# Second convolution buffer, and a new order of the top-k rounds, block adds and sums on VectorE, in a hybrid SSD and sparse attention layer

## The reference, cut to what matters

```python
proj = h @ w_in                                   # (T, 9064)
z, xbc, dt_raw, q, k, v, qi, ki, wi, g = jnp.split(proj, split_points, axis=-1)
xbc, conv_new = causal_conv(xbc, conv_state, conv_w, conv_b)   # 4 taps for each channel
xbc = jax.nn.silu(xbc)
xs, Bm, Cm = jnp.split(xbc, (SSM_INNER, SSM_INNER + SSM_GROUPS * SSM_STATE), axis=-1)
dt = jax.nn.softplus(dt_raw + dt_bias);  A = -jnp.exp(A_log)
y_ssd, ssm_new = ssd_scan(xs, dt, A, Bm, Cm, ssm_state, 64)    # needs the running sums of dt * A
y_ssd = rmsnorm((y_ssd + D_skip * xs) * jax.nn.silu(z), ssm_norm_g)
...
_, sel = lax.top_k(iscore, topk)                  # keys of each query row: 128 or 256
o = softmax(q @ k[sel]) @ v[sel]
...
x = x + (gate_a * (y_ssd @ w_ssm_out) + gate_b * (o @ w_attn_out)) @ w_o
x = x + HierMoE(rmsnorm(x))
```

## Time and profile before

| | us |
|---|---|
| median of 3 runs (1522.3 to 1525.94) | 1523.73 |
| the profiled execution, its own time | 1521.15 |
| its span in the trace | 1519.5 |
| TensorE busy in the span | 1350.7 (89%) |
| VectorE busy | 784.1 (52%) |
| ScalarE busy | 492.6 (32%) |
| GpSimd busy | 229.1 (15%) |

### The profile page before, as it was taken

How to read it: one execution, slowest core, us unless ns; L and a number is a source line. 1 busy time by engine, 2 the same in 40 slices (tenths; PEclk the granted TensorE clock), 3 DMA queues, 4 the chain that set the end, 5 groups by cost and what they waited for, 6 DMA issues and landing times.

```text
span 1519.5 us, 19482 instructions
## 1 busy us (share of the span) xinstructions
PE 1350.7 (89%) x7202; PEld 903.1 (59%) x7202; DVE 784.1 (52%) x1707; ACT 492.6 (32%) x1155; POOL 229.1 (15%) x334
## 2 busy tenths in 40 slices
PE   7989789999999999987788899999999969878880
PEld 5545466666676766765565677777765545444440
DVE  3158877878878878878655621101113533211105
ACT  2143124665654655534655420000002211111112
POOL 3000000220320321222530000000000023222210
PEclk9999999999999999999999999999999979988995
DMA  8412332435444435344019425203215199999975
GB/s 262 121 30 54 85 111 94 135 105 161 135 127 130 145 97 139 107 147 111 17 26 193 156 94 159 56 0 116 106 53 241 65 356 414 415 416 415 414 293 215
DMA packets 148176, 247.45 MB, mean 163 GB/s; under 512 B 39540, under 2 KB 106852, under 8 KB 139156
## 3 DMA queue, kind: packets, MB, share of 16 engines
q1 hardware_dynamic: 137012, 215.10, 42.1%
q0 software_dynamic: 11072, 31.12, 6.0%
HBM read 216.50 MB, written 36.88 MB: 167 GB/s over the span
## 4 chain that ended last, share of the span: by engine, by line
PE 47%; DVE 7%; ACT 3%; issue 3%; DMA 2%; POOL 1%; SPq 0%; DVEq 0%; POOLq 0%; ACTq 0%
PE psum L1413 14%; PE psum L1680 9%; PE psum L662 9%; PE psum L1580 5%; PE psum L1696 4%; PE psum L1417 3%; DVE arena L2277 1%; ACT arena L1993 1%; PE psum L1398 1%; ACT arena L1915 1%; PE psum L1317 1%; DVE arena L2716 1%; PE psum L1362 1%; POOL arena L1116 1%; DMA wring<-in_w_in 1%
## 5 line engine op out<-in xcount | busy, mean ns | idle before, releaser
L662 PE MATMUL psum<-hT,wring 128*128 128x320 f32 x1024 | 296.9, 442 | 29.2 <-DVE arena L627 17.4
L662 PEld LDWEIGHTS psum<-hT,wring 128*128 128x128 f32 x1024 | 195.9, 194 | 116.4 <-DVE arena L627 18.9
L662 PE MATMUL psum<-wring 128*128 128x320 f32 x768 | 218.2, 434 | 0.0
L662 PEld LDWEIGHTS psum<-wring 128*128 128x128 f32 x768 | 146.4, 191 | 61.9 <-issue 1.0
L1417 PE MATMUL psum<-ident,arena 128*128 128x128 f32 (+3 forms) x950 | 139.6, 284 | 41.0 <-ACT arena L1915 11.5
L1417 PEld LDWEIGHTS psum<-ident,arena 128*128 128x128 f32 (+3 forms) x950 | 105.2, 143 | 94.8 <-issue 61.9
L1413 PE MATMUL psum<-arena,wring 128*128 128x320 f32 x512 | 138.1, 431 | 0.0
L1413 PEld LDWEIGHTS psum<-arena,wring 128*128 128x128 f32 x512 | 96.6, 189 | 41.2
L638 ACT ACTIVATE wring<-psum 128x320 f32<-128x320 f32 (+2 forms) x140 | 49.6, 379 | 188.7 <-PE psum L662 178.0
L1680 PE MATMUL psum<-wring,arena 128*64 128x256 f32 x608 | 84.3, 439 | 23.8 <-issue 21.0
L1915 ACT ACTIVATE arena<-psum 128x512 f32<-128x512 f32 (+8 forms) x155 | 71.7, 517 | 83.9 <-PE psum L1417 57.1
(11 more groups left out here) (344 smaller groups left out, 1940.9 us busy)
## 6 DMA issues: line engine op xcount, KB each, us to landing
wring<-in_w SPq DMA_DIRECT2D x38, 1024.0 KB, 21.6
arena<-in_w SPq DMA_DIRECT2D x32, 1024.0 KB, 24.7
wring<-in_w_in SPq DMA_DIRECT2D x25, 1024.0 KB, 5.5
oT<-in_w SPq DMA_DIRECT2D x14, 1024.0 KB, 21.8
hT<-in_w SPq DMA_DIRECT2D x12, 1024.0 KB, 20.5
arena<-a_rows SPq DMA_DIRECT2D x20, 512.0 KB, 4.0
arena<-in_state_ssm SPq DMA_DIRECT2D x16, 512.0 KB, 7.3
out<-arena POOLq DMA_DIRECT2D x16, 512.0 KB, 3.8
```

Of the source, the lines that this page charges most:

```text
L662: ins = nc.tensor.matmul(o[:, 0:TH], wt[:, k, :], rows[:, k, :], start=n in (1, 5, 2) and k == 0, stop=k == 3, skip_group_check=True)
```

## The change

Seven edits stand in it, all in the order or the buffers, none in what is computed:

- The taps of odd tiles j go to a second buffer, the first 664 columns of `xdt` (the scan's product buffer, idle at that time). `conv(u)` waits for `silu(u - 2)` rather than `silu(u - 1)`; the tile j = 1 of groups 1 to 3 waits until the scan of the group before has read `xdt` and its state has been written from there; the first product into `xdt` waits for `silu(5)`.
- `sums_of_a` stands on VectorE directly behind block (0, 0) of x1 in group 0, no longer behind the rounds and adds of x1, and TensorE's products for it stand between the first four and the last three steps of x1. ScalarE's part moves up likewise.
- The pair x0 of group 0 uses bank 5 rather than bank 3 for its steps 1, 6, 7 and 4.
- In `sum_rows` the wait for the indexer's query product stands before the one subtraction that overwrites hT, and no longer ahead of all four.
- The rounds between the adds of q 3 and of x0 of group 0 are gone or behind the adds.
- In the first gates the adds of block (0, 0) come ahead of the rounds, and `sum_weights` of gb 0 behind the first of them.
- The tables of rounds: 39 of 80 are done when group 0 begins (45 before), then 54, 59, 64 and 69 at the ends of the groups (54, 58, 62, 66 before), and 11 in the gates (14 before).

```diff
--- before.py
+++ after.py
@@ -43,9 +43,9 @@
 TOPK_P, TOPK_S = 128, 256
 ROUNDS_P = TOPK_P // 8
 ROUNDS = 3 * ROUNDS_P + TOPK_S // 8
-TOP_Q = (24, 27, 34, 38, 43)
-TOP_GROUP = (45, 54, 58, 62, 66)
-TOP_GATES = (70, 75, 79, ROUNDS)
+TOP_Q = (24, 27, 32, 39)
+TOP_GROUP = (39, 54, 59, 64, 69)
+TOP_GATES = (71, 73, 75, 77, 79, ROUNDS)
 CHUNK = 64
 PAIRS = SMP * AR
 ATT_SCALE = HD ** -0.5
@@ -232,18 +232,20 @@
 def plan_group(b, g):
 
     lo, hi = (0, 1, 2, 3), (4, 5, 6, 7)
-    plan_pair(b, ("x", g, 0), (3, 1, 2), SEVEN[:4])
+    x0_banks = (3 if g else 5, 1, 2)
+    plan_pair(b, ("x", g, 0), x0_banks, SEVEN[:4])
     if g:
         b.add(("yt", g - 1), (0,))
     b.add(("cT", g), (7,))
-    plan_pair(b, ("x", g, 0), (3, 1, 2), SEVEN[4:])
-    plan_pair(b, ("x", g, 1), (0, 1, 2))
+    plan_pair(b, ("x", g, 0), x0_banks, SEVEN[4:])
+    plan_pair(b, ("x", g, 1), (0, 1, 2), SEVEN[:4])
     if g == 0:
         for tt in range(NT):
             b.add(("ac", tt), hi)
             b.add(("ae", tt), hi, readers=2)
         for i in range(2):
             b.add(("ar", i), hi)
+    plan_pair(b, ("x", g, 1), (0, 1, 2), SEVEN[4:])
     plan_pair(b, ("bc", g), (3, 1, 2))
     plan_pair(b, ("z", g, 0), (0, 1, 2))
     b.add(("cO", g, 0), (7,))
@@ -438,6 +440,7 @@
         czero = ebs[:, SMP % 2, 0:2 * P].rearrange("p (u t) -> p u t", u=2)
         dec = ebs[:, SMP % 2, 2 * P:2 * P + 4 * SB].rearrange("p (j b) -> p j b", j=4)
         sout = xdt[:, 1, :]
+        taps = [acc[:, 0, :], xdt.rearrange("p u n -> p (u n)")[:, 0:664]]
         arow = ebs.rearrange("p u n -> p (u n)")[0:HEADS, 0:T]
         mt_f = mt.rearrange("p u n -> p (u n)")
 
@@ -678,12 +681,12 @@
         def sum_rows(dve):
 
             tt_ = nc.vector.tensor_tensor
-            wait_full(dve, ("qiS",))
             tt_(row_sums[0], top_r, top_l, ALU.subtract).then_inc(S["sums_ready"], 1)
             dve.wait_ge(S["sums_ready"], 5)
             tt_(row_sums[1], low_r, row_sums[0], ALU.subtract).then_inc(S["sums_ready"], 1)
             dve.wait_ge(S["sums_ready"], 6)
             tt_(row_sums[2], low_l, row_sums[1], ALU.subtract).then_inc(S["sums_ready"], 1)
+            wait_full(dve, ("qiS",))
             tt_(top_r, low_r, top_r, ALU.subtract).then_inc(S["sums_ready"], 1)
 
         def wait_chunk(pe, key):
@@ -1157,7 +1160,7 @@
                 ins = turn(o[:, 24 * j:24 * (j + 1)], cin[0:24, j, :], 24)
             filled(ins, ("cT", g))
             dense(pe, ("x", g, 0), SEVEN[4:])
-            dense(pe, ("x", g, 1))
+            dense(pe, ("x", g, 1), SEVEN[:4])
             if g == 0:
 
                 pe.wait_ge(S["a_ready"], 1)
@@ -1174,6 +1177,7 @@
                         ins = mm(o[0:HEADS, (tt - 4 * i) * P:(tt - 4 * i + 1) * P], av[:, tt, :],
                                  (cum_p if tt < SMP else cum_s)[:], start=True, stop=True)
                     filled(ins, ("ar", i))
+            dense(pe, ("x", g, 1), SEVEN[4:])
             dense(pe, ("bc", g))
             dense(pe, ("z", g, 0))
 
@@ -1747,9 +1751,9 @@
                 ct = 4 * g + j if j < 4 else 16 + g if j == 4 else 20 + g
                 dst = xsT[:, j, :] if j < 4 else bcT[:, j - 4, :]
                 act.wait_ge(S["conv_done"], 6 * g + j + 1)
-                fn(dst[:, 0:TP], acc[:, 0, 0:TP], ACT.Silu, bias=cb_col[:, ct:ct + 1])
+                fn(dst[:, 0:TP], taps[j % 2][:, 0:TP], ACT.Silu, bias=cb_col[:, ct:ct + 1])
                 fn(dst[:, TP:T].rearrange("p (b q) -> p b q", q=SQ),
-                   acc[:, 0, 512:664].rearrange("p (b q) -> p b q", q=19)[:, :, 3:19], ACT.Silu,
+                   taps[j % 2][:, 512:664].rearrange("p (b q) -> p b q", q=19)[:, :, 3:19], ACT.Silu,
                    bias=cb_col[:, ct:ct + 1]).then_inc(S["xs_ready"], 1)
 
             if g == 0:
@@ -1763,11 +1767,7 @@
                 squares_act(act, g - 1, fn)
             stage_(x1_, 6)
             silu(0)
-            stage_(x1_, 5, 7)
-            if g:
-                gains_act(act, g - 1, fn)
-            silu(1)
-            raws(x1_, 2)
+            stage_(x1_, 5)
             if g == 0:
                 for tt in range(NT):
                     wait_read(act, ("ae", tt), 1)
@@ -1777,6 +1777,11 @@
                 fn(w2v, w2v, ACT.Exp).then_inc(S["a_exp"], 1)
                 copy(("ar", 0), arow[:, 0:512], bank(("ar", 0))[0:HEADS, :])
                 copy(("ar", 1), arow[:, 512:T], bank(("ar", 1))[0:HEADS, 0:P])
+            stage_(x1_, 7)
+            silu(1)
+            if g:
+                gains_act(act, g - 1, fn)
+            raws(x1_, 2)
             stage_(bc, 1)
             silu(2)
             stage_(bc, 6)
@@ -2091,9 +2096,12 @@
                 ct = 4 * g + j if j < 4 else 16 + g if j == 4 else 20 + g
                 dve.wait_ge(S["raw_ready"], u + 1)
                 wait_read(dve, key + (3,))
-                if u:
-                    dve.wait_ge(S["xs_ready"], u)
-                a, r = acc[:, 0, :], raw[:, j % 2, :]
+                if u >= 2:
+                    dve.wait_ge(S["xs_ready"], u - 1)
+                if j == 1 and g:
+                    wait_full(dve, ("yo", g - 1, SMP))
+                    dve.wait_ge(S["sout_written"], 16 * g)
+                a, r = taps[j % 2], raw[:, j % 2, :]
                 link(ts_(a, r[:, 0:664], cw_col[:, 0, ct:ct + 1], None, ALU.mult))
                 for w in range(1, CW):
                     ins = stt(out=a, in0=r[:, w:w + 664], scalar=cw_col[:, w, ct:ct + 1], in1=a, op0=ALU.mult, op1=ALU.add)
@@ -2109,17 +2117,19 @@
                     dve.wait_ge(S["gathered"], u - 1)
                 pair_added(dve, key, block)
 
+            def sums_of_a():
+
+                for tt in range(NT):
+                    wait_full(dve, ("ac", tt))
+                    release(nc.vector.tensor_copy(acv[:, tt, :], bank(("ac", tt))[:, 0:HEADS]), ("ac", tt))
+                    wait_full(dve, ("ae", tt))
+                    wait_read(dve, ("ac", tt))
+                    release(tt_(w2v[:, tt, :], bank(("ae", tt))[:, 0:HEADS], acv[:, tt, :], ALU.subtract), ("ae", tt))
+
             tops = TOP_GROUP[g], TOP_GROUP[g + 1]
             rounds = [tops[0] + (tops[1] - tops[0]) * i // 4 for i in range(5)] if g == 0 else \
-                [tops[0], tops[0], tops[0] + 1, tops[0] + 2, tops[1]]
+                [tops[0], tops[0] + 1, tops[0] + 2, tops[0] + 3, tops[1]]
             for i, (key, nxt) in enumerate(((("x", g, 0), ("x", g, 1)), (("x", g, 1), ("bc", g)), (("bc", g), ("z", g, 0)))):
-                if i == 1 and g == 0:
-                    for tt in range(NT):
-                        wait_full(dve, ("ac", tt))
-                        release(nc.vector.tensor_copy(acv[:, tt, :], bank(("ac", tt))[:, 0:HEADS]), ("ac", tt))
-                        wait_full(dve, ("ae", tt))
-                        wait_read(dve, ("ac", tt))
-                        release(tt_(w2v[:, tt, :], bank(("ae", tt))[:, 0:HEADS], acv[:, tt, :], ALU.subtract), ("ae", tt))
                 conv(key, 2 * i)
                 conv(key, 2 * i + 1)
                 if i == 2 and g:
@@ -2129,6 +2139,8 @@
                         raws_added(nxt, 2 * i + 2, block)
                     else:
                         pair_added(dve, nxt, block)
+                    if block == (0, 0) and i == 0 and g == 0:
+                        sums_of_a()
                     if block == (0, 0):
                         sum_weights(dve, (("bc", g), ("z", g, 0), ("z", g, 1))[i])
                         top(rounds[i], rounds[i + 1])
@@ -2138,6 +2150,8 @@
                     tt = step
                     k = NT * g + tt
                     wait_full(dve, ("xt", g, tt))
+                    if tt == 0:
+                        dve.wait_ge(S["xs_ready"], 6 * (g + 1))
                     if tt >= 2:
                         wait_full(dve, ("yo", g, tt - 2))
                     elif tt == 0 and g:
@@ -2213,16 +2227,18 @@
             for block in ((0, 0), (1, 1), (0, 1)):
                 pair_added(dve, nxt, block)
             if g == GROUPS - 1:
-                sum_weights(dve, ("gb", 0, 0))
                 for i, key in enumerate((("ga", 0, 1), ("gb", 0, 0), ("gb", 0, 1))):
-                    top(TOP_GATES[i - 1] if i else TOP_GROUP[-1], TOP_GATES[i])
                     if i == 2:
                         dve.wait_ge(S["squares_added"], GROUPS)
-                    for block in ((0, 0), (1, 1), (0, 1)):
-                        pair_added(dve, key, block)
+                    pair_added(dve, key, (0, 0))
+                    if i == 0:
+                        sum_weights(dve, ("gb", 0, 0))
+                    top(TOP_GATES[2 * i - 1] if i else TOP_GROUP[-1], TOP_GATES[2 * i])
+                    pair_added(dve, key, (1, 1))
+                    pair_added(dve, key, (0, 1))
                     if i == 0:
                         sum_weights(dve, ("gb", 0, 1))
-                top(TOP_GATES[2], TOP_GATES[3])
+                    top(TOP_GATES[2 * i], TOP_GATES[2 * i + 1])
```

(5 more changed lines are left out.)

## The result

| | before | after |
|---|---|---|
| median of the runs measured together, us | 1524.84 | 1504.12 |
| lowest and highest | 1522.3 to 1527.42 | 1500.83 to 1505.47 |
| the profiled execution, its own time | 1521.15 | 1503.05 |
| its span | 1519.5 | 1501.4 |

The ratio is 0.9865, 95% interval 0.9851 to 0.9879: the change makes the kernel 20.7 us faster. The point forecast was 1503, the range 1496 to 1512. The profiled execution before lies 3.7 us under its median and the one after 1.1 under, so the two traces show less than the medians: 18.1 us.

A forecast was written before the change was run, and what follows sets the result against it. VectorE was taken to set the gain in group 0 and the gates' end, though TensorE is busiest. Terms 14.0 + 3.3 + 3.0 = 20.3 us off 1521.15 give 1500.9 profiled, median 1503.4 from 1523.73; range 1496 to 1512.

The forecast's parts named there:

- Group 0, VectorE: From 177.06 to `xt` of group 0: VectorE loses 15.6 us of waits, pays 1.5 more in the sums, gains 14.1.
- VectorE wins 14, and 14 counts: Group 0: TensorE would win 12.8 + 4.2 us and some smaller waits, but VectorE's 14 sets the gain.
- Groups 1 to 3: Groups 1 to 3: 1.1 us won in each from TensorE's wait of 1.09 at z0, 3.3 in all.
- TensorE keeps the 1.46: Groups 1 to 3: ScalarE's staging of step 5 of bc comes no earlier, so TensorE's 1.46 us wait stays.
- rival B: Groups 1 to 3: GpSimd's squares and `conv(1)` exclude each other, the second buffer buys nothing there; 1508.2 us, chance 0.20.
- The gates: Before the attention: three rounds fewer, 7.9 us, but a load wait of 7.5 for 1.90; gain 3.0 us.
- Let through in full: After the gates: no load starts at a fixed time, so the whole gain of 20.3 us reaches the end.

The follow-up runs named there:

- e2: The changed kernel with one convolution buffer instead of two, so the second convolution waits until silu has read the first; 1524.29 us.
- e3: The kernel before with only the top-k rounds moved out of group 0's q phase and bank 5 for the first x matmuls; 1522.22 us.
- e1: The changed kernel with x0 of group 0 put back to PSUM bank 3 from bank 5; 1506.33 us.
- e5: The changed kernel with the old round tables: four rounds a group instead of five in groups 1 to 3, 14 in the gates instead of 11; 1507.85 us.
- e10: e9 with top-k rounds spread anew: two fewer in group 0, one more in each of groups 1 to 3, one fewer in the gates; 1489.02 us.
- e8: The changed kernel with the first top-k round of groups 1 to 3 between the first and second convolution of x's first pair; 1500.77 us.
- e12: The changed kernel with no edit, measured once more beside the kernel before; 1502.74 us.
- e6: The changed kernel with the weight sums of gb 0, pair 1 moved behind the second lot of rounds in the gates; 1498.15 us.
- e9: The changed kernel with late gb 0, pair 1 sums, group 0's exponentials ahead of the first silu, and a round between convolutions in groups 1 to 3; 1496.59 us.

## Why the prediction was right, point by point

- **Group 0, VectorE, 14.0 of 20.3 us.** From 177.06 to `xt` VectorE took 99.61 us before; after, the same list runs from 178.46 to 264.27, 85.8: 13.8 won, forecast 14.1. The rows agree in detail: the three waits for `silu` are gone, the sums of a wait twice, and TensorE has its new wait at `xt`, 4.82 us where 6 to 7 were forecast. (The working gives 14.1; the sum took 14.0.) The term gives the whole gain to the second buffer, which takes the waits for `silu` away. e2 shows that the buffer carries 6.9 us of it; 6.5 stay without it, and e3 has 4.7 at `xt` from the rounds and the bank alone, though its median is only 2.6 lower. The sentence "VectorE wins 14, and 14 counts" was right in its sum and wrong as a picture: e1 shows TensorE to be the bound until the sums of a, so that delaying it by 1.6 us there costs 3.
- **Not in the forecast: the start.** This execution reaches 178.46 some 1.4 us late (177.06 before). Starts from 92.4 to 95.6 us occur among the kernels traced here (first product of 64x256), also in kernels that are equal up to that point.
- **Groups 1 to 3, 3.3 forecast, 5.0 measured.** The term was TensorE's hole of 1.09 us, three times, and that one is gone. The step that failed is "TensorE keeps the 1.46": in group 2 before, the holes were 1.46 and 1.09, after, one of 0.89 is left, so 1.66 us are won, where the group's gain is 1.8. That step was worked out on VectorE: `conv(1)` at 7.4 us beside the squares (measured 0.56 + 5.61 = 6.2) and a new round at 2.62 lost. But e5 shows that a round fewer in a group gains nothing, its hole is 0.89 as well, and e10 that one more costs under 0.1 us a group: TensorE bounds them. What shortened the first hole was not taken apart.
- **Squares beside `conv(1)` (rival B, 0.20).** Not borne out: the groups gained. (By its own working, 1.5 us later in each of three groups, the term would be 1.2 us lost and not 1.5.) The squares and the taps beside them lasted together 7.25 us, for 5.49 + 2.80 + 0.68 = 8.97 one after the other (the 0.68 is a sum behind the taps, stretched to 1.40). The Trainium skill ("SBUF — State Buffer", section "Who interferes with whom") has the two engines exclude each other for a whole instruction when VectorE reads two SBUF inputs. With records laid end to end that would be an estimate of 8.97, and the trace has 7.25: some 0.4 us less for each of the four squares, as it was 0.3 at 652 (1.75 for 2.06). Whether the lock is a partial one, or whole and held for a little less than the records last, these runs do not tell. Its other half, that a VectorE instruction with one SBUF input and outside the two-port modes stays free, agrees with the MAX8 and the MATCH_REPLACE8 of e8.
- **The gates, 3.0 forecast, 3.3 measured.** The wait for the load of gb 0, pair 1 was 6.38 us (7.5 forecast). In the trace of e12, the same kernel, it was 7.38, and the gates won 2.3, so the 3.3 is good to about 1 us. e6 shows that this wait was the price of the order chosen: without it the gates gain another 5.2. (The prediction's text names this load as that of "gb 1".)
- **Let through in full, 20.3 forecast.** The failed step: "What follows the gates has no load that starts at a fixed time, so I let the whole gain through." 1.1 us are lost at the start of the attention to the lower clock, a coupling that the forecast used for group 0 and left out here. e12 loses the same 1.1; e3 lost 1.8 there and 3.3 by 1130; e8, with the same pause, nothing. Another 1.5 us went in the experts' stretch; from the product of 1130.10 (1110.43 after) to the end the fourteen traces take 389.1 to 393.8 us with the same instructions: 389.4 before, 391.0 after, but 389.6 in e12. So two executions of the changed kernel differ there by 1.4 us, and the 1.5 are no effect of the change that the traces show. The two longest are those of e10 and e9, the earliest to arrive; whether that is more than the spread of executions stays open.

The balance of the two traces: 13.8 + 5.0 + 3.3 = 22.1 us won, 1.4 + 1.1 + 1.5 lost, 18.1 left, which is the difference of the spans. The medians show 20.7. That 1503.4 came so close is partly luck: the groups' term, sized too small, stood against losses that were not priced, and the forecast took the execution profiled before to lie 2.6 us under the median, where the later measurement has 3.7. For the profiled execution itself it had 1500.9, measured 1503.05.

## What to carry to other kernels

For each stretch, first find the engine whose list has no waits that matter, and price an edit on that engine alone; the same filling work (here a top-k round of 2.6 us) is free in one stretch and costs its full length in another, so move it to where it is free. A stretch can change its bound halfway, at a point where two engines hand over, and slack behind that point is not slack ahead of it. Behind a load, time saved ahead of the wait only lengthens the wait, unless the wait itself is moved later. And a pause of TensorE can be paid twice, in the pause and in the slower clock that follows; here the same pause of 3.77 us cost 1.1 us more in one kernel and nothing in another.
